# A decoder step in fp32: weights in five single-piece buffers, and V pages four at a time in column strips

## The reference

```
z = rmsnorm(x) @ w_in                       # one projection for all branches and gates
A = Bg * dwconv3(Cg * h)                    # short gated convolution
B = gated DeltaNet, 4 heads, chunks         # a chain of small 128x128 products
C = layernorm/silu of a 31-tap convolution
D = forgetting attention, 8 heads of 64     # samples: over 16 pages of 128 keys each
x += (sum_i sigmoid(gate_i) * (o_i @ w_branch_i)) @ w_out
x += cross attention over a memory of 256
x += (silu(dwconv3(xn W_g)) * (xn W_u)) @ W_d
y = rmsnorm(x)
```

## Time and profile before

| | |
|---|---|
| time, median of 3 runs | 1883.24 us (1877.06 to 1886.03) |
| time of the profiled execution | 1885.36 us |
| its span (first to last instruction) | 1883.5 us |
| TensorE busy | 1612.5 us (86%) |
| VectorE, GpSimd, ScalarE busy | 876.8, 633.5, 560.5 us |
| TensorE's granted clock, mean | 0.911 of full |
| moved by DMA | 200.02 MB, 106 GB/s over the span |

### The profile page before, as it was taken

How to read it: one execution, slowest core, us unless ns; L and a number is a source line. 1 busy time by engine, 2 the same in 40 slices (tenths; PEclk the granted TensorE clock), 3 DMA queues, 4 the chain that set the end, 5 groups by cost and what they waited for, 6 DMA issues and landing times. The chain is left out here.

```text
span 1883.5 us, 28308 instructions
## 1 busy us (share of the span) xinstructions
PE 1612.5 (86%) x11064; PEld 1417.9 (75%) x11064; DVE 876.8 (47%) x1334; ACT 560.5 (30%) x903; POOL 633.5 (34%) x354
## 2 busy tenths in 40 slices
PE   4999899876686678998896899898677999999996
PEld 3899677766575577664343899897566899999995
DVE  4004777777986765313222122255334566664021
ACT  3334232235101322211115223345213333333222
POOL 1337444333466662110000344330402344443341
PEclk8999899877778898999998999999767899999998
DMA  6225322232245442444443522323212222222231
GB/s 196 78 80 176 95 91 96 79 101 90 89 124 179 129 131 67 133 137 140 128 153 102 177 86 78 123 91 101 101 67 68 68 90 90 90 94 82 88 115 46
DMA packets 154389, 200.02 MB, mean 106 GB/s; under 512 B 10180, under 2 KB 112125, under 8 KB 153848
## 3 DMA queue, kind: packets, MB, share of 16 engines
q1 hardware_dynamic: 137253, 169.46, 28.4%
q10 hardware_dynamic: 16011, 24.02, 3.7%
q0 software_dynamic: 992, 4.72, 0.8%
HBM read 187.92 MB, written 10.94 MB: 106 GB/s over the span
## 5 line engine op out<-in xcount | busy, mean ns | idle before, releaser
L740 POOL TENSOR_TENSOR wl<-raw,wh 128x1024 fp32r<-128x1024 f32 (+2 forms) x196 | 427.1, 2179 | 1096.1 <-ACT wh L1105 1094.6
L779 PE MATMUL pb<-xh,wh 128*128 128x260 f32 x2176 | 644.7, 296 | 37.0 <-DVE xl L1480 22.4
L779 PE MATMUL pb<-xl,wh 128*128 128x260 f32 x2176 | 629.8, 289 | 0.0
L779 PE MATMUL pb<-xh,wl 128*128 128x260 f32 x2176 | 628.1, 289 | 0.0
L779 PEld LDWEIGHTS pb<-xh,wh 128*128 128x128 f32 x2176 | 424.7, 195 | 54.7 <-issue 43.3
L779 PE MATMUL sd<-ar 128*128 128x128 f32 (+7 forms) x1584 | 361.4, 372 | 80.0 <-DVE ar L1480 24.7
L779 PEld LDWEIGHTS pb<-xl,wh 128*128 128x128 f32 x2176 | 425.4, 196 | 0.5
L779 PEld LDWEIGHTS pb<-xh,wl 128*128 128x128 f32 x2176 | 425.0, 195 | 0.0
L1105 ACT ACTIVATE wh<-raw 128x1024 fp32r<-128x1024 f32 (+2 forms) x208 | 201.6, 969 | 557.3 <-PE pb L779 530.5
L779 PEld LDWEIGHTS sd<-ar 128*128 128x128 f32 (+4 forms) x1584 | 209.3, 196 | 199.1 <-issue 135.4
L751 POOL TENSOR_TENSOR ar<-ar 128x512 f32<-128x512 f32 x128 | 178.3, 1393 | 95.3 <-DMA ar<-in_cache_fox_k 65.1
(11 more groups left out here) (163 smaller groups left out, 1691.0 us busy)
## 6 DMA issues: line engine op xcount, KB each, us to landing
raw<-in_w_in SPq DMA_DIRECT2D x40, 1024.0 KB, 5.4
ar<-in_cache_fox_k SPq DMA_DIRECT2D x128, 256.0 KB, 2.8
ar<-in_cache_fox_v SPq DMA_DIRECT2D x128, 256.0 KB, 2.8
raw<-in_w_ffn_in SPq DMA_DIRECT2D x22, 1024.0 KB, 5.1
raw<-in_w_branch SPq DMA_DIRECT2D x16, 512.0 KB, 3.5
raw<-in_w_ffn_out SPq DMA_DIRECT2D x8, 1024.0 KB, 5.4
ar<-in_cache_mem_k ACTq DMA_DIRECT2D x1, 4096.0 KB, 19.9
raw<-in_w_out SPq DMA_DIRECT2D x4, 1024.0 KB, 5.2
```

The lines of the kernel that those rows point to most:

```text
L740: pool.tensor_tensor(wl[:, p % 2, 0:kt, :], raw[:, u % 2, 0:kt, half * P:(half + 1) * P], wh[:, p % 2, 0:kt, :].bitcast(F32), SUB).then_in ...
L779: return pe.matmul(o, l, r, start=start, stop=stop, skip_group_check=True)
```

## The change

**The weights.** Units are no longer loaded as such. SP loads each piece by itself (128 columns, 512 KB, rows of 512 bytes) into one of five buffers (`RING` 5), four pieces ahead; the load for piece p + 4 stands at piece p and waits until TensorE is done with piece p - 1. High parts go to three buffers and are made two pieces ahead (`AHEAD` 2). The low part is written in place, over the raw weights (`rawl`).

**The V pages.** They are loaded and multiplied four at a time (`VG` 4), in two groups of four buffers, the second where branch C's output was. Page j of a group writes rows 32j to 32j + 7 of the bank, so each has its own strip of 32 columns of TensorE's array. One group is put before a side step instead of two pages (`V_STEP` 1). After the fourth group of a sequence VectorE multiplies the bank by a mask (`own_head`) that keeps, in the 8 rows of each strip, the head's own 64 columns. One event later ("vx") four matmuls of the 128 x 128 blocks of that product by a column of ones add up strips and heads, and VectorE copies the 4 columns to `vo`. The scratch, its stores and reads, and step ("df", 0) are gone.

```diff
@@ -128,6 +128,7 @@
+RING, AHEAD = 5, 2
@@ -155,7 +156,8 @@
-V_FILLED, V_BARE = 2, 2
+V_STEP = 1
+VG = 4
@@ -437,8 +440,10 @@
-        raw = sb("raw", [P, 2, KD, 256])
-        wh, wl = sb("wh", [P, 2, KD, P], F32R), sb("wl", [P, 2, KD, P], F32R)
+        raw_at = -(-nc.sbuf_base // 32) * 32
+        raw = sb("raw", [P, RING, KD, P])
+        rawl = nc.alloc_sbuf_tensor_at("rawl", [P, RING, KD, P], F32R, offset=raw_at)
+        wh = sb("wh", [P, AHEAD + 1, KD, P], F32R)
@@ -671,41 +681,49 @@
                 sp.dma_start(bias[:, 16:20], a["gdn_a_log"].to_broadcast([P, 4])).then_inc(small_in, 16)
-            def unit(u):
-
+            def weights(p):
+
+                u, half = PIECES[p][:2]
                 w, row, kt, c = UNITS[u]
-                if u >= 2:
-                    sp.wait_ge(lo.sem, 2 * u - 2)
-                sp.dma_start(raw[:, u % 2, 0:kt, :], W[w][row:row + kt * P, c:c + 256].rearrange("(k p) n -> p k n", p=P))\
-                    .then_inc(raw_in[u % 2], 16)
-
-            def page(cache, i):
+                c += half * P
+                if p >= RING:
+                    sp.wait_ge(piece_done.sem, p - RING + 1)
+                sp.dma_start(raw[:, p % RING, 0:kt, :], W[w][row:row + kt * P, c:c + P].rearrange("(k p) n -> p k n", p=P))\
+                    .then_inc(raw_in[p % RING], 16)
+
+            def page(cache, i, to, landed):
...
                 n = sp.value_load(ptr_[0:1, i:i + 1], min_val=0, max_val=a[cache].shape[0] - 1)
-                sp.dma_start(kring[:, i % 4, :], a[cache][bass.ds(n, 1)].rearrange("a p l h d -> (a p) (l h d)"))\
-                    .then_inc(page_in[i % 4], 16)
-
-            unit(0)
-            unit(1)
+                sp.dma_start(to, a[cache][bass.ds(n, 1)].rearrange("a p l h d -> (a p) (l h d)")).then_inc(landed, 16)
+
+            def k_page(i):
+                page("cache_fox_k", i, kring[:, i % 4, :], page_in[i % 4])
+
+            def v_group(g):
+                for i in range(VG * g, VG * g + VG):
+                    page("cache_fox_v", i, v_slot(i), v_in[i % 8])
+
+            for p in range(RING - 1):
+                weights(p)
             sp.wait_ge(pt_in, 32)
             for i in range(3):
-                page("cache_fox_k", i)
+                k_page(i)
             for e in TIMELINE:
-                if e[0] == "piece" and e[2] == 1 and PIECES[e[1]][1] == 0 and PIECES[e[1]][0] + 2 < len(UNITS):
-                    unit(PIECES[e[1]][0] + 2)
+                if e[0] == "piece" and e[2] == 0 and e[1] + RING - 1 < NP_:
+                    weights(e[1] + RING - 1)
                 elif e[0] == "k" and e[1] + 3 < N_PAGE:
...
                         sp.wait_ge(page_free.sem, e[1])
-                    page("cache_fox_k", e[1] + 3)
+                    k_page(e[1] + 3)
                 elif e[0] == "vstart":
...
                     sp.wait_ge(pe_s.sem, upto(pe_works, ITEMS.index(("dc", 1)) + 1))
-                    for i in range(3):
-                        page("cache_fox_v", i)
-                elif e[0] == "v" and e[1] + 3 < N_PAGE:
+                    sp.wait_ge(sp_lo.sem, KB)
+                    v_group(0)
+                elif e[0] == "v" and VG * (e[1] + 1) < N_PAGE:
                     if e[1] >= 1:
                         sp.wait_ge(v_used.sem, e[1])
-                    page("cache_fox_v", e[1] + 3)
+                    v_group(e[1] + 1)
@@ -750,10 +768,11 @@
-            split(0)
+            for p in range(AHEAD):
+                split(p)
             for e in TIMELINE:
-                if e[0] == "piece" and e[2] == 0 and e[1] + 1 < NP_:
-                    split(e[1] + 1)
+                if e[0] == "piece" and e[2] == 0 and e[1] + AHEAD < NP_:
+                    split(e[1] + AHEAD)
                 elif e[0] == "k":
@@ -873,9 +892,9 @@
-                    mm(o, wh[:, p % 2, k, :], xa, first and k == 0, False)
-                    mm(o, wh[:, p % 2, k, :], xb, False, False)
-                    last = mm(o, wl[:, p % 2, k, :], xa, False, last_ and k == kt - 1)
+                    mm(o, wh[:, p % (AHEAD + 1), k, :], xa, first and k == 0, False)
+                    mm(o, wh[:, p % (AHEAD + 1), k, :], xb, False, False)
+                    last = mm(o, rawl[:, p % RING, k, :], xa, False, last_ and k == kt - 1)
@@ -1074,14 +1090,24 @@
-            def page(i):
-
-                if i == 0:
+            def v_group(g):
+
+                if g == 0:
                     pe.wait_ge(dve_s.sem, upto(dve_works, ITEMS.index(("ds", 3)) + 1))
-                elif i % PAGES == 0:
-                    pe.wait_ge(v_rows.sem, i // PAGES)
-                pe.wait_ge(page_in[i % 4], 16 * (N_PAGE // 4 + i // 4 + 1))
-                v_used.by(mm(s3[0:FH, :], sc[:, i, :], kring[:, i % 4, :], i % PAGES == 0, i % PAGES == PAGES - 1))
+                elif g % V_OF == 0:
+                    pe.wait_ge(v_out.sem, g // V_OF)
+                for j in range(VG):
+                    i = VG * g + j
+                    pe.wait_ge(v_in[i % 8], 16 * (i // 8 + 1))
+                    last = mm(s3[32 * j:32 * j + FH, :], sc[:, i, :], v_slot(i), g % V_OF == 0, g % V_OF == V_OF - 1)
+                v_used.by(last)
+
+            def v_heads(b):
+
+                pe.wait_ge(v_rows.sem, b + 1)
+                for c in range(KB):
+                    last = mm(s3[:, c:c + 1], vdiag[:, c * P:(c + 1) * P], ones[:, 0:1])
+                v_sum.by(last)
@@ -1106,13 +1134,11 @@
-                u, half, kt = PIECES[p][:3]
-                if half == 0:
-                    act.wait_ge(raw_in[u % 2], 16 * (u // 2 + 1))
-                if p >= 2:
-                    act.wait_ge(piece_done.sem, p - 1)
-                    act.wait_ge(lo.sem, p - 1)
-                fn(wh[:, p % 2, 0:kt, :], raw[:, u % 2, 0:kt, half * P:(half + 1) * P], ACT.Copy, hi)
+                kt = PIECES[p][2]
+                act.wait_ge(raw_in[p % RING], 16 * (p // RING + 1))
+                if p > AHEAD:
+                    act.wait_ge(piece_done.sem, p - AHEAD)
+                fn(wh[:, p % (AHEAD + 1), 0:kt, :], raw[:, p % RING, 0:kt, :], ACT.Copy, hi)
@@ -1446,20 +1473,6 @@
-                elif e[0] == "v" and e[1] % PAGES == PAGES - 1:
-                    b = e[1] // PAGES
-                    act.wait_ge(v_used.sem, e[1] + 1)
-                    if b >= 2:
-                        act.wait_ge(vs_out[b % 2], 16 * (b // 2))
-                    fn(vrow[0:FH, b % 2, :], s3[0:FH, :], ACT.Copy, v_rows)
-                    at = b * FH * (512 + FD)
-                    store(vscr[at:at + FH * 512].rearrange("(h n) -> h n", h=FH), vrow[0:FH, b % 2, :], vs_out[b % 2])
-                    if b == NB - 1:
...
-                        for j in range(2):
-                            act.wait_ge(vs_out[j], 16 * NB // 2)
-                        for j in range(2):
-                            act.dma_start(v64[0:NB * FH, j, :], vscr.rearrange("(r n) -> r n", n=512 + FD)[:, 0:FD]).then_inc(v64_in, 16)
@@ -1832,7 +1845,7 @@
-                        tt(o, o, s3[r, 0:64].rearrange("p (b c t) -> p c b t", b=NB, t=2)[:, :, :, j], ADD)
+                        tt(o, o, vo[r, :, :], ADD)
@@ -1892,6 +1905,7 @@
+            red(own_head, ident.rearrange("p (j r) -> p r j", r=32)[:, 0:FH, :], ADD)
@@ -1917,12 +1931,19 @@
                     tap(e[1])
-                elif e[0] == "piece" and e[2] == 0 and e[1] + 1 < NP_:
-                    split(e[1] + 1)
+                elif e[0] == "piece" and e[2] == 0 and e[1] + AHEAD < NP_:
+                    split(e[1] + AHEAD)
                 elif e[0] == "k" and e[1] > 0:
...
                     reduce_page(N_PAGE - 1)
+                elif e[0] == "v" and e[1] % V_OF == V_OF - 1:
+                    dve.wait_ge(v_used.sem, e[1] + 1)
+                    v_rows.by(dve.tensor_tensor(vdiag.rearrange("p (h d) -> p h d", h=FH), s3.rearrange("p (h d) -> p h d", h=FH),
+                                                spread(own_head, FD, 2), MUL))
+                elif e[0] == "vx":
+                    dve.wait_ge(v_sum.sem, e[1] + 1)
+                    own(dve.tensor_copy(vo[:, :, e[1]], s3[:, 0:KB]), v_out)
```

More of the change, by code:

```diff
@@ L198, in adds_before, with step @@
     return sum(KD - 1 for n in ADDED if n < i)
+MARKS = ("AFTER", "BEFORE", "TAPS", "REDUCES", "KSTART", "VSTART", "PAGES")
+N_TAP = KB * CFW
 N_PAGE = PAGES * NB
+V_OF = PAGES // VG
+V_EVENTS = [x for b in range(NB) for x in [("v", V_OF * b + n) for n in range(V_OF)] + [("vx", b)]]
 def timeline():
     out, pos, step_n, tile, at_piece, bg = [], [0], [0], [0], [-1], {"tap": None, "k": None, "v": None}
-    size = {"tap": N_TAP, "k": N_PAGE, "v": N_PAGE}
+    size = {"tap": N_TAP, "k": N_PAGE, "v": len(V_EVENTS)}
     def background(kind, n):
-        for done in range(n):
+        for _ in range(n):
             if bg[kind] is not None and bg[kind] < size[kind]:
-                if kind == "v" and bg[kind] % PAGES == 0 and done > 0 and n < 10:
-                    return
```

(28 more changed lines are left out.)

26 lines of the change are left out of this document (12 added, 14 removed).

## The result

The changed kernel takes 1888.5 us (median of 20 runs, 1880.2 to 1898.3) against 1882.3 for the kernel before (1877.1 to 1886.7): a ratio of 1.0031, 95% interval 1.0017 to 1.0045. I had said 1855. The profiled execution has a span of 1889.3 us against 1883.5.

What follows compares the result with a forecast made beforehand. TensorE, busy 86% of the span, was taken as the bound. Terms +5 + 5.5 - 6.5 - 11.8 - 20 = -27.8 took the 1883.2 us median to 1855, with an 8-in-10 range of 1830 to 1893.

Steps and rivals of the forecast that it cites:

- Four pages in column strips: V pages on TensorE: eight instructions overlap partly, in 5 slots, 2.1 us a group; bounds 1.0 and 3.4 us.
- second rival: V pages: four strips run in one span, 1.0 us a group, total -45, 1838 us; chance 0.18.
- The join: Per sequence, VectorE multiply, heads' matmuls and copy set against the removed row copy: nothing, bounds +-1 us for each of five.
- late first load: Stage 1: the first V group's pages stand behind piece 72's weights, so TensorE waits some 3 us.
- Later groups are asked for two events ahead and fit: Stage 1: V loads after the first group are requested over 7 us ahead and arrive in time.
- fourth rival: V stage: loads late by 2 to 3 us on a dozen groups, +25 on the forecast, 1880 us; chance 0.10.
- Stage 2: 833 to 920.25 us, end of chunk 1 and chunk 2: pairs of 7.5 us, badly placed multiply +2; +5.5, bounds -9 and +29.
- stage 1: 752 to 833 us, projection pieces and V pages sharing TensorE: +5, bounds -8 and +22.
- Stage 3: 920.25 to 995.14 us, chunk 3: bare chain, 6.0 us pairs, -14.5; lower clock +8; sum -6.5, bounds -15 and -1.
- wrong in the main: Signs of failure: groups over 2.9 us, load waits group after group, or clock near one half throughout chunk 3 (+17).
- Stage 4: 995.14 to 1027.23 us, normalizing steps: V pages and scratch round trip go, -11.8; result's VectorE work under 11 us of pieces.
- The ring: Weights' buffers: -6 for 1.00 us waits, -8 in memory's K/V projection, -6 in K stage; -20, bounds -8 and -26.

Runs made afterwards that it cites:

- e9: Changed kernel with a sequence's last V group and heads' matmuls allowed only before odd delta-rule steps (3 to 15) and 16: 1860.1 us, ratio 0.9893.
- e3: Changed kernel plus idle 128x128 matmuls before chunk 3's delta-rule steps from step 1 on and before four normalizing steps: 1878.3 us, ratio 0.9973.
- e1: Kernel before with the change's weights' ring alone, V pages as before: 1875.9 us, ratio 0.9966.
- e11: e10 with the low parts of the memory's K/V weights made by GpSimd instead of VectorE: 1839.4 us, ratio 0.9780.
- second pair: Changed kernel with a sequence's last V group only before even delta-rule steps, without and with idle matmuls (the latter is e6): 1872.8 and 1863.9 us.
- e10: e9 plus idle 128x128 matmuls from chunk 2 on where no group or heads precede a step, 18 before a normalizing step: 1844.9 us, ratio 0.9800.
- e6: Changed kernel with a sequence's last V group only before even delta-rule steps, plus idle matmuls from chunk 2 on: 1863.9 us, ratio 0.9898.

## Why the prediction was wrong, step by step

- **Four pages in column strips, 2.1 us a group.** Measured 1.04. My argument that a page's second instruction can't be passed, and so makes 5 slots, was wrong; the second rival's mechanism is what happens. The Trainium skill (TensorE: Matmul & The Clock Gate, Part 3: Packing small matmuls) says that matmuls in different column groups run at once, and by 1.04 us in four strips against 3.60 in one the trace agrees. But the rival's 1838 did not come with it, since that rival too had the join at nothing, and no late loads in chunk 2.
- **The join, "at nothing" with one badly placed multiply at +2.** This was the largest error. Left out, the kernel is 31 us faster. In the right order (e9) the kernel is 28 us faster by the medians with the join in; part of that is fewer groups in the early stages, so what the join costs in the right order stays open. I had priced the heads on TensorE and asked who waits for the rows, but not what stands behind the multiply in VectorE's queue. The stage to chunk 2 went up by 7.4 us where I had +5 up to 833 us. Three waits for VectorE, 10.2 us together, are more than that. The late first load that I had named came as well, and with the size that I gave it (0.95 us of wait and 2.8 of stretch, for my 3).
- **"Later groups are asked for two events ahead and fit."** In chunk 2 they don't. 16 groups and the joins took 82.6 us, against 66.3 without loads, and nearly all of that is stretch inside the groups (32.6 us against 18.3). It is my fourth rival, for the shorter groups: its mechanism was there, together with the second's.
- **Stage 2, +5.5.** With stage 1 I had +10.5 for all up to chunk 3. It was +7.4 + 10.6 = +18.0, by multiply and loads, not by pairs of 7.5 us. (Its own terms, 2.2 + 2 + 1, make 5.2 and not 5.5; and stage 1's lower bound of -8 is about -6 by the case that it names.)
- **Stage 3, -14.5 for the bare chain and +8 for the clock.** The chain was right: pairs of 6.04 at the full clock in e3, and chunk 3 at 63.1 us against the 74.9 - 14.5 = 60.4 of the sum. The clock term was too small. Chunk 3 was 78.0, +3.1. That is the case that I had named as wrong in the main (a clock near one half, +17): -14.5 + 17 = +2.5. I had taken 0.8 where the nearest row, from 1330 to 1393 us, had 0.70 at a like busy share.
- **Stage 4, -11.8.** The round trip is gone, and up to the point that I had priced the term was nearly right: from the first normalizing matmul to piece 76 it is 32.4 us before (995.14 to 1027.50) and 22.7 after (1016.04 to 1038.74), -9.7, with no wait ahead of the piece. Behind it 5.5 us are lost again, from piece 76 to the memory's transposes (27.0 before, 32.5 after), so -4.1 is left. There VectorE's work on the result, which I had put under the pieces, is in the way: the first export waits 4.30 us for it. The clock costs here too: e3 has 27.1 us for gp against 30.9.
- **The ring, -20.** The six waits of 1.00 us are gone, and their stretch gave 7.8 us where I had 6 (5.3 in e1): right in cause and nearly in size. The K/V projection gave 1.1 of 8: part of the cause was VectorE's low part, as e11 shows. The K stage gave nothing of 6: TensorE reached the V stage at 738.4 us after and at 738.65 before, and between 733.9 and 741.7 in the runs with the ring, 737.4 in the mean. The three waits for GpSimd (3.90, 3.38 and 4.54 us) became three for ScalarE at the same places:

```profile
482.85 0.36 PE L798 MATMUL pb<-xh,wh 128*128 128x260 f32 x1 [2.76 <-ACT ar L1133]
494.33 0.56 PE L798 MATMUL pb<-xh,wh 128*128 128x260 f32 x1 [3.97 <-ACT ar L1133]
618.91 0.36 PE L798 MATMUL pb<-oh,wh 128*128 128x260 f32 x1 [2.40 <-ACT ar L1133]
```

ScalarE had itself stood 7.85 us waiting for VectorE just before the first of them (at 480.28). That this is what holds the stage is read from the rows, not tested.

By size, the forecast's -27.8 missed by 34 us: 7.5 in the stages up to chunk 3, 9.6 in chunk 3, 7.7 in stage 4, 9 in the ring. The measured 1888.5 lies inside the range of 1830 to 1893, but that is luck: the range reached up there for the sake of groups of 3.4 us, and the groups took 1.04. What stays open is how loads and join share chunk 2, since no run left out both.

## What to carry to other kernels

When an operation is added to an engine's queue, look at what stands behind it and when the input of that work was ready; an operation of 0.7 us in an idle engine cost 2.6 to 4.5 us in each of three places, since it waited for TensorE ahead of work that didn't have to. Work that makes TensorE faster in a chain of waits can lower its clock and slow down all the rest; price the chain at the lower clock first, and if gaps are left, matmuls of constants in them may pay (10, 9 and 15 us by the medians of three pairs of kernels here; in the second pair chunk 3 itself got no shorter). When a consumer gets more than three times as fast, work out the bandwidth that it then asks for before counting the gain.

## What the runs showed of the hardware that I had not expected

- Four fp32 matmuls of 128x512 (two instructions each) in four strips of 32 columns take 1.04 us, as long as one page alone (1.02 us); in one strip 3.60 us.
- TensorE busy 48.9 of 78 us in chunk 3 got a granted clock of 0.63; 52.2 of 72.6 us in e9 0.81; 61.1 of 66.2 us in e10 1.00. Matmuls whose result nobody reads count as work for it: with them e3's chunk 3 got 0.97. The busy share alone doesn't give the clock: 55.4 of 63.1 us in e3 and 65.4 of 74.3 us in e6 are both 88%, at 0.97 and 0.89.
- A wait for a load can hide from TensorE's own rows: 2.7 us there, and leaving out the loads gave 18 us. The length of the groups showed it (32.6 us for 16 in chunk 2, 18.3 without loads); the weight-load queue's waits (20.8 us) don't rank kernels by it, since e10 has 22.8.
